# Second layer's experts: eleven load slots for the weights in place of seven, and the side work taken in pairs

## The reference, cut to what matters

```python
y = (silu(x @ w_gate[e]) * (x @ w_up[e])) @ w_down[e]      # x: 64 x 1024, each weight 1024 x 1024, fp32
```

## Time and profile before

| | us |
|---|---|
| median of three runs | 2769.12 |
| profiled execution | 2769.65 |
| its span | 2767.8 |
| PE busy | 2560.1 (92%) |
| DVE busy | 1313.0 (47%) |
| ACT busy | 1002.7 (36%) |
| POOL busy | 355.4 (13%) |
| DMA moved | 567.72 MB, 205 GB/s over the span |

### The profile page before, as it was taken

One profiled execution on the slowest core, in us unless ns is written; L12 is line 12 of the kernel. 1 busy time (PEld: TensorE's weight loads), 2 busy tenths in 40 slices (PEclk: granted clock), 3 DMA queues, 4 the chain that ended last, 5 costly groups with the idle time before them and its releaser, 6 DMA issues.

```text
span 2767.8 us, 35477 instructions
## 1 busy us (share of the span) xinstructions
PE 2560.1 (92%) x13952; PEld 1517.2 (55%) x13952; DVE 1313.0 (47%) x2565; ACT 1002.7 (36%) x1859; POOL 355.4 (13%) x190
## 2 busy tenths in 40 slices
PE   6999987899999997997869999998999898999998
PEld 3875566432332222774644333332667787788887
DVE  2497545344444444677452333333754654443342
ACT  4216642344444344535432222222443334322222
POOL 0220002001111101220100000000223221122221
PEclk9999999899999998999989999999999899999999
DMA  6216733599999998210129999999120002223221
GB/s 253 67 59 246 282 113 122 227 354 378 375 372 374 369 369 314 103 67 1 38 99 421 421 409 409 388 407 377 34 89 31 12 17 96 84 93 105 92 84 54
DMA packets 85452, 567.72 MB, mean 205 GB/s; under 512 B 11744, under 2 KB 12000, under 8 KB 20264
## 3 DMA queue, kind: packets, MB, share of 16 engines
q1 hardware_dynamic: 79128, 547.01, 50.8%
q0 software_dynamic: 3616, 11.80, 1.9%
q10 hardware_dynamic: 2544, 6.66, 0.7%
HBM read 550.74 MB, written 14.68 MB: 204 GB/s over the span
## 4 chain that ended last, share of the span: by engine, by line
PE 45%; DVE 4%; DMA 1%; ACT 1%; issue 1%; DVEq 0%; ACTq 0%
PE PS L1015 12%; PE PS L1115 4%; PE PS L1113 4%; PE PS L1114 4%; PE PS L1127 3%; PE PS L1128 3%; PE PS L1129 3%; PE PS L1073 3%; PE PS L1103 2%; PE PS L786 1%; PE PS L1239 1%; PE PS L1244 1%; PE PS L1159 1%; PE PS L1145 1%; DMA X<-in_w_up_dram 1%
## 5 line engine op out<-in xcount | busy, mean ns | idle before, releaser
L2637 POOL TENSOR_TENSOR WHL<-RING,WHL 128x1024 fp32r<-128x1024 f32 x64 | 172.8, 2700 | 1514.5 <-ACT WHL L1360 1514.5
L1015 PE MATMUL PS<-RING,RF 128*64 128x512 f32 x1448 | 342.2, 601 | 3.9 <-ACT RF L1615 1.0
L1015 PE MATMUL PS<-WIDE,RF 128*64 128x512 f32 x1408 | 328.8, 600 | 1.3 <-ACT RF L1596 0.6
L1360 ACT ACTIVATE WHL<-RING 128x1024 fp32r<-128x1024 f32 x129 | 134.6, 1047 | 216.1 <-PE PS L1129 130.7
L1113 PE MATMUL PS<-RR,WHL 128*128 128x512 f32 x512 | 205.8, 402 | 1.8 <-DVE RR L2390 1.8
L1015 PEld LDWEIGHTS PS<-RING,RF 128*64 128x64 f32 x1448 | 92.8, 136 | 208.7 <-issue 198.6
L1115 PE MATMUL PS<-RR,WHL 128*128 128x512 f32 x512 | 203.5, 397 | 0.0
L1114 PE MATMUL PS<-RR,WHL 128*128 128x512 f32 x512 | 202.0, 394 | 0.0
L1015 PEld LDWEIGHTS PS<-WIDE,RF 128*64 128x64 f32 x1408 | 94.0, 137 | 196.2 <-issue 184.9
L1615 ACT ACTIVATE RF<-PS,MODS,MSC 128x128 f32<-128x128 f32 x192 | 74.5, 439 | 243.0 <-PE PS L1073 147.0
L1868 DVE TENSOR_TENSOR WHL<-RING,WHL 128x1024 fp32r<-128x1024 f32 x65 | 79.5, 1224 | 173.8 <-ACT WHL L1360 167.7
(11 more groups left out here) (382 smaller groups left out, 4825.1 us busy)
## 6 DMA issues: line engine op xcount, KB each, us to landing
RING<-in_w_gate_dram SPq DMA_DIRECT2D x83, 1024.0 KB, 7.5
WIDE<-in_w_down_dram SPq DMA_DIRECT2D x74, 1024.0 KB, 7.9
RING<-in_w_up_dram SPq DMA_DIRECT2D x70, 1024.0 KB, 5.9
WIDE<-in_w_up_dram SPq DMA_DIRECT2D x57, 1024.0 KB, 8.2
RING<-in_w_down_dram SPq DMA_DIRECT2D x51, 1024.0 KB, 8.6
RING<-in_ada_w_dram SPq DMA_DIRECT2D x48, 1024.0 KB, 6.3
WIDE<-in_w_gate_dram SPq DMA_DIRECT2D x45, 1024.0 KB, 8.1
RING<-in_w_in_dram SPq DMA_DIRECT2D x30, 1024.0 KB, 4.9
```

The lines of the kernel that those rows point to most:

```text
L1015: ins = e.matmul(a[r:r + 64, :], xs[:, j, 0:64], w[:, i, :], start=j < 2, stop=j > 5)
L1360: e.activation(h, load_buffer(ld)[:, js, cs], ACT.Copy).then_inc(act, A(("hi", st["i"])))
L2637: e.tensor_tensor(lo, load_buffer(loads[st["load"]])[:, js, cs], h.bitcast(F32), ALU.subtract).then_inc(pool, G(("lo", st["i"])))
```

## The change

Three things change, all for the second layer's experts:

- The 188 loads turn over eleven slots, 7, 8, 9, 4, 5, 6, 10, 0, 1, 2, 3. Four new ones lie in the work memories `RF` and `AR`, in parts that are free from the end of attention (7, 8, 9) or from the last split weight of the output projection (10). The small work tiles (`picked_tokens`, `hidden`, `UP`, `DN`) move within `RF` to make room.
- The last of the 188 loads falls on slot 7 in place of slot 2, so the first loads of `w_in2` (slots 0, 1, 2) follow on slots that the steps 4, 3 and 2 before the last one leave, not on those of the last three.
- `aside(q)` takes the place of `pump()`: in the second layer no side item after the first step of a product and two after the second.

```diff
@@ weight_steps
-            ld["slots"] = (4, 5, 6, 0, 1, 2) + (3,) * l
+            ld["slots"] = (7, 8, 9, 4, 5, 6, 10, 0, 1, 2, 3) if l else (4, 5, 6, 0, 1, 2)
...
-        ld.update(slot=k, n=count[k], before=last.get(k), after=split if k > 3 else None)
+        ld.update(slot=k, n=count[k], before=last.get(k), after=split if k in (4, 5, 6, 10) else None)
...
-                wide = st["i"] if k > 3 else wide
+                wide = st["i"] if k in (4, 5, 6) else wide
@@ experts_plan
+    def aside(q):
+
+        for _ in range(1 if need_ctx else (0, 2)[q]):
+            pump()
...
-                        pump()
+                        aside(q)
...
-                    pump()
+                    aside(q)
@@ program
-        weights_in = [sem(f"weights_in{i}") for i in range(NRING + 4)]
+        weights_in = [sem(f"weights_in{i}") for i in range(NRING + 8)]
...
+            elif ld["slot"] < NRING + 4:
+                b = WIDE[:, ld["slot"] - NRING - 1, :]
             else:
-                b = WIDE[:, ld["slot"] - NRING - 1, :]
+                b = (rf(8192, 2048), rf(10240, 2048), ar(4096, 2048), rf(6144, 2048))[ld["slot"] - NRING - 4]
...
-            return rf(3072 + 768 * (e % 2), 8, n_)
+            return rf(32 * n_ + 8 * n_ * (e % 2), 8, n_)
...
-        UP = [rf(4608, 512), rf(5120, 512)]
+        UP = [[rf(4608, 512), rf(5120, 512)], [rf(3072, 512), rf(3584, 512)]]
...
-        DN = [rf(7680, 512), rf(8192, 512)]
+        DN = [[rf(7680, 512), rf(8192, 512)], [rf(4096, 512), rf(4608, 512)]]
@@ sync
                 elif ld["slot"] == NRING:
                     e.wait_ge(dve, V["hn", "1a", 5])
+                elif ld["slot"] in (7, 8, 9):
+                    e.wait_ge(pe, P["pv", 1, 31])
```

More of the change, by code:

```diff
@@ L664, in picked_tokens @@
         def picked_tokens(g, n_):
-            return rf(1536 * (g % 2), 8, 2, n_)
+            return rf(16 * n_ * (g % 2), 8, 2, n_)
         def hidden(e, n_):
-            return rf(3072 + 768 * (e % 2), 8, n_)
+            return rf(32 * n_ + 8 * n_ * (e % 2), 8, n_)
         GX, GC = ar(0, 1024), ar(1024, 1024)[0:64, :]
-        UP = [rf(4608, 512), rf(5120, 512)]
+        UP = [[rf(4608, 512), rf(5120, 512)], [rf(3072, 512), rf(3584, 512)]]
         CT, CU = [rf(5632, 512), rf(6144, 512)], [rf(6656, 512), rf(7168, 512)]
-        DN = [rf(7680, 512), rf(8192, 512)]
+        DN = [[rf(7680, 512), rf(8192, 512)], [rf(4096, 512), rf(4608, 512)]]
         CD, CE = [rf(8704, 512), rf(9216, 512)], [rf(9728, 512), rf(10240, 512)]
@@ L1559, in experts @@
                             e.wait_ge(dve, V["h", l, i - 2])
-                        dst = UP[i % 2] if w else HE[i % 3]
+                        dst = UP[l][i % 2] if w else HE[i % 3]
                         e.activation(dst[0:64, :], held("upA", l, ex, half, w)[64:128, :], ACT.Copy
@@ L1595, in experts @@
                                 e.wait_ge(dve, V["given", l, i - 2])
-                            e.activation(DN[i % 2][0:64, :], held("downA", l, ex, half)[64:128, :], ACT.Copy
+                            e.activation(DN[l][i % 2][0:64, :], held("downA", l, ex, half)[64:128, :], ACT.Copy
                                          ).then_inc(act, A(("dnA", l, i)))
@@ L2291, in experts @@
                         n = 2 * i + w
-                        dst, c = (UP[i % 2] if w else HE[i % 3])[0:64, :], CT[n % 2][0:64, :]
+                        dst, c = (UP[l][i % 2] if w else HE[i % 3])[0:64, :], CT[n % 2][0:64, :]
                         e.wait_ge(act, A["lowA", l, n])
@@ L2304, in experts @@
                         e.wait_ge(act, A["low2", l, n])
-                        e.tensor_tensor((UP[i % 2] if w else HE[i % 3])[64:96, :], CT[n % 2][0:32, :], CU[n % 2][0:32, :],
+                        e.tensor_tensor((UP[l][i % 2] if w else HE[i % 3])[64:96, :], CT[n % 2][0:32, :], CU[n % 2][0:32, :],
                                         ALU.add).then_inc(dve, V(("ctx", l, n)))
@@ L2312, in experts @@
                         e.wait_ge(dve, V["ctx", l, 2 * i + 1] if need_ctx else V["upA", l, ex, half, 1])
-                        e.tensor_tensor(ho, ho, UP[i % 2][0:n_, :], ALU.mult).then_inc(dve, V(("h", l, i)))
+                        e.tensor_tensor(ho, ho, UP[l][i % 2][0:n_, :], ALU.mult).then_inc(dve, V(("h", l, i)))
                     elif what == "result":
@@ L2317, in experts @@
                         a0, z = 64 * (ex % 2), slice(512 * half, 512 * half + 512)
-                        dn, c = DN[i % 2][0:64, :], CD[i % 2][0:64, :]
+                        dn, c = DN[l][i % 2][0:64, :], CD[i % 2][0:64, :]
                         if stage == 0:
```

## The result

| | before | changed |
|---|---|---|
| median, us | 2769.12 (five runs, 2768.45 to 2779.23) | 2749.64 (five runs, 2745.17 to 2756.51) |
| ratio of the runs | | 0.9923, 95% interval 0.9907 to 0.994 |
| span of the profiled execution | 2767.8 | 2747.8 |

The changed kernel is faster by 0.77%, 21 us (17 to 26) by the ratio and 19.5 by the medians. 15.4 were forecast. In a second set of runs on another occasion the ratio was 0.9899 (0.9883 to 0.9915). The parts of the forecast fare differently from their sum: one term was three times too small, another three times too large.

What follows compares the result with a forecast made beforehand. The prediction took the experts' stretch as bound by PE on the whole, and by loads where many steps come without side items. Savings of 5.3 + 5.3 + 4.8 = 15.4 us gave 2753.7 us, range 2748 to 2763.

Steps and rivals of the forecast that it cites:

- The waits for loads: Experts' stretch: four more slots remove both clusters of PE's waits for loads, -5.3 us, bounds 0 and 5.6.
- The side items in pairs: Experts' stretch: pairing saves 0.08 us per two picks, 0.15 per two sends, -5.3 us in all.
- Eight picks in a row take 9.00, or 1.12 each: PE's timeline: price of a pick before a pick, 1.12 us, set beside 1.06 to 1.09 before a step.
- The way back into the steps: PE from side item to step: nothing on the pick's side, about 0.05 us on the step's side.
- The exit: PE leaving the steps for a side item: costs 0.15 us each; 50 fewer exits are 7.5 us.
- Rival 3: More than forecast: both borders cost 0.15 us (2744), or the clock stays up (about 2752); chance 0.07.
- The end: Behind the experts' last step: `w_in2` is issued 4.9 us earlier, the chain shifts whole, -4.8 us, bounds 0 and 7.3.
- nothing is ahead of it: `w_in2`'s load near the experts' end: no other load queues before it, so landing takes 5.2 us at most.
- Rival 4: Experts' stretch: loads bind again, stalls and late `w_in2` stay, only the pairs' 5.3 us remain, 2763.8 us; chance 0.08.
- The figure from memory: Expert loads: a skill page's 358 GB/s would make a load 2.9 us and the DMA bind throughout; rejected for 421 GB/s.
- Rival 5: Pairs wait for their own evictions from the side ring; slower, 2775.7 us at 0.45 us a pair; chance 0.04.
- Rivals 1 and 2: 1: the end doesn't move, another wait ends last, 2758.5 us, chance 0.11; 2: pairs worth nothing, 2759.0 us, chance 0.10.

Runs made afterwards that it cites:

- the slots alone: The changed kernel with its old order, one side item after each step, so eleven slots without pairs: 2759.38 us, ratio 0.9956 against the kernel before.
- the two kernels without any wait for a load: Eleven slots with single side items (2759.38 us), and the changed kernel with slot 0 moved to the end of the turn and `w_in2` on slots 1, 2, 0 (2745.47 us).
- the pairs alone: The kernel before, seven slots kept, with no side item after a product's first step and two after its second: 2758.73 us, ratio 0.9952.
- the late split: The changed kernel with the first two splits of `w_in2` moved behind the last expert's results on ACT, DVE and POOL: 2743.21 us, ratio 0.9902.
- the version with the early restart: The changed kernel with slot 0 last in the turn, `w_in2` on slots 1, 2, 0, and its first two splits behind the last expert's results: 2741.03 us, ratio 0.9897.

## Why the prediction was right and wrong

**The waits for loads** (5.3 us forecast). Right in mechanism and, with the slots alone, in size: 5.8 us. In the changed kernel 2.3 us of them come back (1.9 printed, 0.4 of run-out), in the second cluster, because PE is faster than was forecast. "All but the flip's go" was wrong by that much.

**The side items in pairs** (5.3 us forecast). This is the step that failed. With eleven slots T - S falls from 483.1 to 468.0, 15.1 us, though 2.3 us of waits for loads have come back with it: 17.4 us of PE's work, three times the term; the two kernels without any wait for a load give 17.4 as well. The fault is in one reading: "Eight picks in a row take 9.00, or 1.12 each". The same eight picks of the kernel before by windows, with the clock in the column before the DMA share:

```profile
1426.00:1428.00 2.00, 1.69 (x8) 1.72 (x9) 0.95 (x5) 0.00 (x0) 0.00 (x0) 0.50 0.00 0
1428.00:1430.00 2.00, 2.00 (x12) 2.00 (x12) 0.00 (x0) 0.47 (x2) 0.00 (x0) 0.57 0.00 0
1430.00:1432.00 2.00, 2.00 (x20) 2.00 (x19) 0.00 (x0) 1.13 (x3) 0.00 (x0) 1.00 0.01 4
```

and what comes behind them:

```profile
1435.15 0.60 PE L786 MATMUL PS<-CON,AR 128*128 128x128 f32 x4
```

For the first 3.4 us PE ran at half its clock (0.50, its 1.2 GHz level), having just stood still. 12 instructions fall into the second window, most of it at half the clock, and 20 into the third, at the full one. By distance the eight take 1435.15 - 1426.31 = 8.84 us; less the 1.7 us that the half clock cost, 7.14, or 0.89 each. So 1.12 us was a mean over two clocks, set beside the 1.09 of a pick at the full clock, and the two nearly agreed by accident. At the full clock a pick in front of a pick takes 0.89 us, in front of a step 1.09. The way back into the steps, which the forecast took as free on the pick's side, costs 0.20 us there, besides the 0.05 on the step's side that the forecast had. The exit, forecast at 0.15, is some 0.10 (a step behind a step takes 1.72, and 1.82 if a pick follows; behind a pick 1.77, and 1.87). So a pair of picks saves 0.20 + 0.05 + 0.10 = 0.35 us, the 5.92 - 5.57 of the timeline. For sends it is 5.84 - 5.50 = 0.34: two together take 1.92. Their three in a row had been read as 3.03, which is a duration; by distance those of 1906.45 to 1909.42 in the same trace take 2.97. That is still 0.99 each, 0.03 more than 0.96; whether the third waits for a bank of the side ring is not shown.

The forecast had the alternative in hand. The rule of the Trainium skill, TensorEngine Tiling, section Tiling Modes, that a change of tiling mode drains the TensorE, spares no direction; the estimate by it was 15 us for both borders. The case's runs give 17.4 and side with the rule on this: both borders have a price. What the array does at them no run shows. Rival 3, which carried it with 0.07 together with a better clock, was the nearest in its mechanism (the clock fell all the same, to 0.50); its 2744 us left out what the stream of loads would take back.

**The end** (4.8 us forecast). Right with the slots alone (5.0), too large in the changed kernel (1.6). `w_in2`'s issue moved as forecast, and the chain behind its landing did shift whole. What failed is "nothing is ahead of it" and with it the landing "5.2 us at most": it took 8.42, since the pairs bring T down to the stream's own end. Rival 4's mechanism, the loads binding again because PE uses up the lead, came true in part, for 2.3 + 3.2 us. The prediction argued against it with PE's pace of 2.60 us against 2.49 of the stream; the pace became 2.49.

**The sum.** By distances: 10.8 us for the slots alone, 11.4 for the pairs alone, 22.1 for both. That these add up is not because the edits are independent: each alone removes one limit and meets the other (9.1 us of idle time before steps with the pairs alone; PE's work with the slots alone). Where the stream binds, the four more loads that lie ready at its restart are worth 4 x 2.49 = 10 us, and T - S fell by 477.9 - 468.0 = 9.9. That this is near the 10.8 us of stalls and end where PE binds is chance.

**The figure from memory.** The Trainium skill, SBUF — State Buffer, section Summary: rules for kernel authors, would by the prediction's estimate have one load take 2.9 us; the trace holds 421 GB/s from 1500 to 1900, in which the stream now never pauses, so 2.49.

**The range.** The median, 2749.64, is inside 2748 to 2763; the time that follows from the ratio, 2747.8, is just under it. That the sum came so near is partly luck: 12 us too little for the pairs, and 5.0 us too much for the loads and the end, which the pairs themselves used up. Rival 5 did not show: no side item waits for an eviction within a pair. Rivals 1 and 2 did not either: with the slots alone the end did move, and the pairs are worth more, not nothing.

## What to carry to other kernels

Before a duration is taken as a price, look at the granted clock of that very stretch: a run of instructions that follows a pause mixes two clocks, and a mean over both can look like a plausible third value. Where two resources are nearly level, work out for each term whether it still counts once the other terms have been paid: what PE gives up beyond the spare pace of the DMA comes back as waits, here 5.5 of some 28 us. And gather small full-array items between column-tiled products, anywhere in the product; both borders cost, and what comes next in the order of a shared queue or engine (a load that waits for the fourth step, a split in front of the last result) can be worth a good part of the edit itself: 6.0 and 7.5 us here, 8.7 together, beside 22.1.

## What was not expected of the hardware

- The same pause of PE, 2.2 us, left the clock at 1.00 over the sends that followed in the late split (7.70 us), and in the version with the early restart it fell to 0.50 behind the pause (9.20 us). After 8.3 us of pause they took 10.30, at 0.50 for some 5 us. In the kernel before the clock was at 0.51 3.2 us into its pause.
- DVE's multiplication at L2350 takes 0.69 us, but 2.74 where it starts beside POOL's split, in the kernel before and in every kernel that keeps that order; in the late split, where POOL's split comes behind it, it takes 0.70.
- Loads into other memories than before (`RF`, `AR`), from which PE reads both operands of a matmul, showed no price: steps on them take 1.72 us as those on `RING` and `WIDE`.
